# Six-layer transformer on one core: the 96 modulation slots move from TensorE to VectorE

## The reference, cut to what matters

```python
def _adaln(c, w, b):
    mod = jax.nn.silu(c) @ w + b        # (1,2048) @ (2048, 6144), for each of two layers
    shift, scale, gate = jnp.split(mod, 3, axis=-1)
```

## Time and profile before

| | |
|---|---|
| time, median of 3 runs (lowest, highest) | 4247.78 us (4247.11, 4262.5) |
| span of the profiled execution, first to last instruction | 4257.0 us |
| time of that execution outside its span | not listed |
| busy: PE, PE weight load, DVE, ACT, POOL | 3822.6, 3641.7, 2778.6, 2089.6, 599.0 us |
| mean granted TensorE clock | 0.950 of full speed |
| HBM read | 676.25 MB, 159 GB/s over the span |

### The profile page before, as it was taken

How to read it: one execution, slowest core, us unless ns; L and a number is a source line. 1 busy time by engine, 2 the same in 40 slices (tenths; PEclk the granted TensorE clock), 3 DMA queues, 4 the chain that set the end, 5 groups by cost and what they waited for, 6 DMA issues and landing times.

```text
span 4257.0 us, 80674 instructions
## 1 busy us (share of the span) xinstructions
PE 3822.6 (90%) x29682; PEld 3641.7 (86%) x29682; DVE 2778.6 (65%) x4250; ACT 2089.6 (49%) x3218; POOL 599.0 (14%) x564
## 2 busy tenths in 40 slices
PE   7999998988889886798999989889999897899997
PEld 6898888877779886798989889788989886799996
DVE  6676665566666675566667666678787774754555
ACT  5555544555545546555555544444454443443442
POOL 1011012100002201122101111223121221100000
PEclk9999999999999987899999999899999998899998
DMA  5555544444444432344555444343434342244442
GB/s 211 188 206 190 187 169 155 162 178 169 176 152 176 150 139 100 141 168 159 198 187 198 186 161 178 138 149 138 160 136 157 143 151 95 109 168 160 161 167 89
DMA packets 93571, 681.56 MB, mean 160 GB/s; under 512 B 10401, under 2 KB 10529, under 8 KB 11169
## 3 DMA queue, kind: packets, MB, share of 16 engines
q1 hardware_dynamic: 92880, 676.75, 43.6%
q0 software_dynamic: 464, 1.64, 0.1%
HBM read 676.25 MB, written 2.10 MB: 159 GB/s over the span
## 4 chain that ended last, share of the span: by engine, by line
PE 60%; DVE 15%; issue 10%; ACT 9%; POOL 4%; DVEq 1%; ACTq 0%; DMA 0%; POOLq 0%; SPq 0%
PE g L336 18%; PE g L337 17%; PE g L338 17%; DVE w_lo L1263 5%; ACT w_hi L789 4%; POOL scratch L2052 3%; PE norm_bank L349 1%; PE g L396 1%; PE g L395 1%; DVE scratch L1759 1%; ACT scratch L829 1%; ACT scratch L828 1%; PE turn_bank L375 1%; DVE scratch L1325 1%; PE g L408 1%
## 5 line engine op out<-in xcount | busy, mean ns | idle before, releaser
L1263 DVE TENSOR_TENSOR w_lo<-w_raw,w_hi 128x1024 fp32r<-128x1024 f32 x1280 | 1578.8, 1238 | 936.1 <-ACT w_hi L789 933.2
L789 ACT ACTIVATE w_hi<-w_raw 128x1024 fp32r<-128x1024 f32 x1280 | 1322.9, 1053 | 1328.4 <-PE g L338 1310.9
L336 PE MATMUL g<-p_hi,w_hi 128*128 128x256 f32 x4624 | 1346.8, 291 | 59.0 <-DVE scratch L1669 17.2
L337 PE MATMUL g<-p_lo,w_hi 128*128 128x256 f32 x4624 | 1324.3, 286 | 0.0
L338 PE MATMUL g<-p_hi,w_lo 128*128 128x256 f32 x4624 | 1323.5, 286 | 0.0
L336 PE MATMUL g<-q_hi,w_hi 128*128 128x256 f32 x3472 | 1004.5, 289 | 51.4 <-DVE q_lo L1833 14.8
L337 PE MATMUL g<-q_lo,w_hi 128*128 128x256 f32 x3472 | 991.4, 286 | 0.0
L338 PE MATMUL g<-q_hi,w_lo 128*128 128x256 f32 x3472 | 991.3, 285 | 0.0
L336 PEld LDWEIGHTS g<-p_hi,w_hi 128*128 128x128 f32 x4624 | 902.1, 195 | 74.3 <-DVE w_lo L1263 39.8
L337 PEld LDWEIGHTS g<-p_lo,w_hi 128*128 128x128 f32 x4624 | 903.4, 195 | 1.0
L338 PEld LDWEIGHTS g<-p_hi,w_lo 128*128 128x128 f32 x4624 | 902.8, 195 | 0.0
(11 more groups left out here) (339 smaller groups left out, 3750.8 us busy)
## 6 DMA issues: line engine op xcount, KB each, us to landing
w_raw<-in_slots SPq DMA_DIRECT2D x640, 1024.0 KB, 4.8
h<-in_x SPq DMA_DIRECT2D x1, 2048.0 KB, 10.9
out_h<-h SPq DMA_DIRECT2D x1, 2048.0 KB, 6.3
scratch<-in_p POOLq DMA_DIRECT2D x4, 256.0 KB, 3.8
con<-in_consts SPq DMA_DIRECT2D x1, 878.0 KB, 4.9
scratch<-in_distance POOLq DMA_DIRECT2D x1, 576.0 KB, 4.0
vec<-in_vecs SPq DMA_DIRECT2D x1, 383.0 KB, 3.2
scratch<-in_positions SPq DMA_DIRECT2D x1, 128.0 KB, 6.5
```

What stands on the lines that cost most here:

```text
L336: pe.matmul(g, wh, hi[:, k], start=n == 0, stop=False)
L337: pe.matmul(g, wh, lo[:, k], start=False, stop=False)
L789: act.activation(w_hi[k % SPLIT][:, cols], raw[k % RAW][:, cols], ACT.Copy).then_inc(hi_ready, 1)
L1263: dve.tensor_tensor(w_lo[k % SPLIT][:, cols], raw[k % RAW][:, cols], w_hi[k % SPLIT][:, cols], SUB).then_inc(lo_ready, 1)
```

## The change

The modulation slots are no longer split and PE no longer touches them. DVE multiplies each of the 8 pieces of a raw slot by the matching column of `silu(c)` (one value per partition) and sums them into `acc` over 128 partitions (`ada_half`: four pieces each, all but the slot's last linked to the next). `mod_columns` on PE sums over the partitions and now waits for `ada_summed`. In an A head, each even tick has its first half before the take and its second half at the end of the tick. In a B pair, slot 0 stands behind `b_weigh`, slot 1 ahead of the first `mod_columns`, slot 2 behind `b_y_lo`, slot 3 ahead of the take of the second gate tile. The raw buffers are handed out in the order main, main, modulation (A) and main, main, modulation, modulation (B). A load still waits for what was in its buffer before: for `lo_ready` after an ordinary slot, for `ada_used` after a modulation slot. `c_silu` replaces `ada_hl` and `ada_hz`; one short preparation step on ACT and two on DVE go. `lo_half` indexes raw buffers as `hi_ahead` does, the loop counts and the counts in GpSimd's list follow; those are left out here.

```diff
@@ -292,17 +333,57 @@
-        n_slots = t["slots"].shape[0]
-        for s in range(RAW):
-            sp.dma_start(raw[s][:], t["slots"][s]).then_inc(landed[s], 16)
-        c.k["slot"] = RAW
-        with c.loop(sp, "slots", 1, n_slots // RAW) as i:
+        kinds = []
+        def load(index, kind="main"):
+            s = c.k.get("raw", 0) % RAW
+            if len(kinds) >= RAW:
+                if kinds[-RAW] == "main":
+                    sp.wait_ge(lo_ready, c.at("slot", -kinds[1 - RAW:].count("main")) * 2)
+                else:
+                    sp.wait_ge(ada_used, c.at("ada", -kinds[1 - RAW:].count("ada")))
+            sp.dma_start(raw[s][:], t["slots"][index]).then_inc(landed[s], 16)
+            kinds.append(kind)
+            c.next("raw")
+            c.next("slot" if kind == "main" else "ada")
+        def run(first, n):
             for s in range(RAW):
-                sp.wait_ge(lo_ready, c.at("slot", -RAW + 1) * 2)
-                sp.dma_start(raw[s][:], t["slots"][i * RAW + s]).then_inc(landed[s], 16)
-                c.next("slot")
+                load(first + s)
+            if n >= 2 * RAW:
+                with c.loop(sp, "run", 1, n // RAW) as i:
+                    for s in range(RAW):
+                        load(i * RAW + (first + s))
+            for s in range(n // RAW * RAW, n):
+                load(first + s)
+        def a_head(at):
+            for main, ada in zip((0, 3, 6, 9), (1, 4, 7, 10)):
+                load(at + main)
+                load(at + main + 2)
+                load(at + ada, "ada")
+        def b_pair(at):
+            for two in (0, 4):
+                load(at + two + 1)
+                load(at + two + 3)
+                load(at + two, "ada")
+                load(at + two + 2, "ada")
+        def heads(first):
+            a_head(first)
+            with c.loop(sp, "a_heads", 1, A_HEADS) as i:
+                a_head(i * 12 + first)
+        heads(0)
+        run(96, 34 + 9)
+        b_pair(139)
+        with c.loop(sp, "b_pairs", 1, B_PAIRS) as i:
+            b_pair(i * 8 + 139)
+        run(203, 34 + 36 + 34)
+        heads(307)
+        run(403, 34 + 113 + 88 + 2)
...
@@ -381,31 +462,14 @@
             w = slot()
             tile(w, range(SLOT), hi, lo, range(SLOT), arriving=arriving)
-        def mod_slot(m, fresh=False):
-            w = slot()
-            pe.wait_ge(tile_taken, c.at("tile", 0 if fresh else -1))
-            g = G[c.bank][0:2, 0:SEQ]
-            c.bank ^= 1
-            for b in range(8):
-                if b == 4:
-                    second_half()
-                k = 8 * (m % 2) + b
-                cols = slice(b * SEQ, (b + 1) * SEQ)
-                pe.matmul(g, ada_hl[:, k], w_hi[w][:, cols], start=b == 0, stop=False)
-                last = pe.matmul(g, ada_hz[:, k], w_lo[w][:, cols], start=False, stop=b == 7)
-                if b == 3:
-                    last.then_inc(half_used, 1)
-            last.then_inc(tile_done, 1)
-            c.next("tile")
         def mod_columns():
-            pe.wait_ge(tile_taken, c.at("tile"))
+            pe.wait_ge(ada_summed, c.next("ada_sum"))
+            pe.wait_ge(tile_taken, c.at("tile", -1))
             g = G[c.bank]
             c.bank ^= 1
             for e in range(2):
-                last = pe.matmul(g[:, e:e + 1], acc[0:2, e * P:(e + 1) * P], K("ones", 1, rows=2), start=True, stop=True)
+                last = pe.matmul(g[:, e:e + 1], acc[:, e * P:(e + 1) * P], K("ones", 1), start=True, stop=True)
             last.then_inc(tile_done, 1)
             c.next("tile")
...
@@ -478,8 +542,6 @@
                         pe.matmul(bS[s][:, 0:P], q[:, 0:P], k[:, 0:P], start=True, stop=True)
                         pe.matmul(bS[s][:, P:3 * P], q[:, P:SEQ], k, start=True, stop=True).then_inc(scored, 1)
                     c.next("score_read", 2)
-                if j % 2 == 0:
-                    mod_slot(j // 2)
                 if j in (3, 7):
                     mod_columns()
...
@@ -499,11 +561,9 @@
         def b_pair(hi, lo, prev):
             c.bank = 0
-            mod_slot(0, fresh=True)
             w = slot()
             for n in range(3):
-                tile(w, range(4 * n, 4 * n + 4), c_hi, c_lo, range(4))
-            mod_slot(1)
+                tile(w, range(4 * n, 4 * n + 4), c_hi, c_lo, range(4), fresh=n == 0)
             if prev:
                 b_turn_weights()
             norm_pair(K("avg_128"), [bsq[:, 0], bsq[:, 1]])
...
@@ -514,12 +574,10 @@
             if prev:
                 b_mix()
             mod_columns()
-            mod_slot(2)
             rotate(bq[:, 2], K("swap_64"), 3)
             norm_pair(K("avg_128"), [bsk[:, 0], bsk[:, 1]])
             square_tiles(hi, lo)
             turn([bv[:, s, n * P:(n + 1) * P] for s in range(2) for n in range(2)], tile_taken, c.at("tile", -1))
-            mod_slot(3)
             square_tiles(hi, lo)
             mod_columns()
             pe.wait_ge(roped, c.next("roped"))
...
@@ -782,11 +840,13 @@
         def hi_ahead(half, ahead=2):
-            k = c.k["slot"] + ahead - 1
+            k, r = c.k["slot"] + ahead - 1, c.k["raw"] % RAW
             cols = slice(half * HALF, (half + 1) * HALF)
             if half == 0:
-                act.wait_ge(landed[k % RAW], c.fours("slot", ahead - 1) * 16)
-            act.activation(w_hi[k % SPLIT][:, cols], raw[k % RAW][:, cols], ACT.Copy).then_inc(hi_ready, 1)
+                act.wait_ge(landed[r], c.fours("raw", 0) * 16)
+            act.activation(w_hi[k % SPLIT][:, cols], raw[r][:, cols], ACT.Copy).then_inc(hi_ready, 1)
+            if half == 1:
+                c.next("raw")
         def factor_pair():
             act.wait_ge(factor_ready, c.at("norm"))
...
@@ -884,6 +944,8 @@
         def a_head(y, i, prev, first):
             for j in range(8):
+                if j % 2 == 0:
+                    c.next("raw")
                 tick(read=True)
                 if j < 4:
                     act.activation(sqh[:, j % 2], qs[:, j % 3], ACT.Square).then_inc(sq_head, 1)
...
@@ -905,8 +967,6 @@
                     sigmoid(zc[:, j - 6], clamped, c.next("clamped"))
                 if j == 7:
                     a_softmax()
-                if j % 2 == 0:
-                    tick()
                 if j in (3, 7):
                     c.next("tile")
...
@@ -936,11 +996,10 @@
             turned(b_sm[:, 1], bR[:, 0:384])
         def b_pair(y, i, prev):
-            tick()
+            c.next("raw", 2)
             tick(3, read=True)
             for n in range(3):
                 squares(bsq[:, n], bq[:, n])
-            tick()
             if prev:
                 b_turned()
             factor_pair()
...
@@ -1273,16 +1330,31 @@
             c.bank ^= 1
             return g
-        def mod_tick(m):
-            begin()
-            g = take()[0:2]
-            if m % 2 == 0:
-                dve.tensor_copy(acc[0:2], g).then_inc(tile_taken, 1)
-            else:
-                dve.wait_ge(tile_taken, c.at("tile", -1))
-                dve.tensor_tensor(acc[0:2], acc[0:2], g, ADD).then_inc(tile_taken, 1)
-            lo_half(1)
+        def ada_next():
+            at = c.k["raw"] % RAW, c.fours("raw", 0) * 16
+            c.next("raw")
+            return at
+        def ada_half(at, m, half):
+            r, value = at
+            if half == 0:
+                dve.wait_ge(landed[r], value)
+            for b in range(4 * half, 4 * half + 4):
+                w = raw[r][:, b * SEQ:(b + 1) * SEQ]
+                k = 8 * (m % 2) + b
+                if k == 0:
+                    last = dve.tensor_scalar(acc[:], w, c_silu[:, 0:1], None, MUL)
+                else:
+                    last = dve.scalar_tensor_tensor(acc[:], w, c_silu[:, k:k + 1], acc[:], MUL, ADD)
+                if b < 7:
+                    link(last)
+            if half == 1:
+                last.then_inc(ada_used, 1)
+                dve.wait_ge(ada_used, c.next("ada"))
+                if m % 2:
+                    dve.sem_inc(ada_summed, 1)
         def mod_columns(i, at):
             two = lambda base: bass.ds(i * 4 + (base + at), 2)
...
@@ -1383,7 +1455,11 @@
         def a_head(y, i, prev, first, jl):
             for j in range(8):
+                if j % 2 == 0:
+                    ada = ada_next()
                 begin()
+                if j % 2 == 0 and not (first and j == 0):
+                    ada_half(ada, j // 2, 0)
                 g = take()
                 if first and j == 0:
                     factor()
...
@@ -1430,7 +1506,9 @@
                         last = dve.tensor_reduce(tiny[:, 5 + 2 * s:6 + 2 * s], sm[:, s, P:384], AX.X, MAX, negate=True)
                     last.then_inc(maxed, 1)
                 if j % 2 == 0:
-                    mod_tick(j // 2)
+                    if first and j == 0:
+                        ada_half(ada, 0, 0)
+                    ada_half(ada, j // 2, 1)
                 if j in (3, 7):
```

(25 more changed lines are left out.)

60 lines of the change are left out of this document (48 added, 12 removed).

## The result

| | before | after |
|---|---|---|
| median (lowest, highest) of 4 runs each | 4252.98 us (4247.11, 4262.5) | 4382.12 us (4377.64, 4384.88) |
| ratio, 95% interval | | 1.0302 (1.0282 to 1.0322) |
| span of the profiled execution | 4257.0 us | 4382.6 us |
| mean granted TensorE clock | 0.950 | 0.917 |

The change makes the kernel 129 us slower. The page after: span, busy times, the chain by engine, and two groups, the linked multiply-adds and ACT's copies; they answer to the earlier trace rows.

The account below looks back on a forecast made before the run. PE was taken to bound A heads, and the order of waits between PE and DVE to bound B pairs. A +40, B +93 and preparation -1 gave +132 us on 4247.8: 4380 us, range 4270 to 4480.

Parts of the forecast that it names:

- A +40: All A heads together: 14 at +3 us each, less 2 us for the layers' first heads, +40 us.
- B +93: Eight B pairs, each +11.6 us longer than the 49.4 us before: +93 us.
- the pair's 61: Period of a B pair: 56.2 us at full clock, 61 with low clock behind PE's waits; bounds 55 and 66.
- the low clock: B pair: slower PE work behind three waits adds 1.5, 1.2 and 2.5 us on the path.
- What is removed: PE loses 1.9 us a modulation slot, 7.7 an A head, 7.3 a B pair; an A head needs PE 57.2 us.
- 8 x 0.63 = 5.0 us: DVE's cost per modulation slot: eight linked multiply-adds at layer C's linked pace of 0.63 us, 5.0 us.
- Rival (b): Links between DVE's multiply-adds cost nothing, 3.2 us a slot: about 4216 us; chance 0.07.
- Forecast waits of DVE: A head: behind exponentials 2.9, load 3.6, rotation 1.5, half of slot 4 3.7 to 4.9, load for slot 8 1.3 us.
- the raw buffers bite too: B pair: next queries' load queues behind a modulation slot's load; DVE idles from 29.2 to 35.9 us.
- (a): Whole kernel: PE is relieved and DVE keeps up, 182 us less, 4066 us; chance 0.06.
- (c): Loads hide and the clock holds: A head 62.9, B pair 56.5 us, +25 us, 4273 us; chance 0.2.
- (d): Low clock also behind every A head's 5 us wait and before its next slot 0: 4477 us; chance 0.12.

Follow-up runs that it names:

- e_early: Changed kernel with A's raw buffers ordered main, modulation, main, and one modulation half ahead of each tick's split in A heads: 4239.48 us, ratio 0.9962.
- e_twochain: Changed kernel with two interleaved sums, each multiply-add awaiting the one before the last, and mod_columns adding both: 4323.55 us, ratio 1.0162.
- e_order: Changed kernel with raw buffers in the A layers alone handed out main, modulation, main: 4294.52 us, ratio 1.0098.
- e_bwarm2: Changed kernel with useless matmuls ahead of PE's three waits in each B pair, the third batch reaching up to the scores: 4328.82 us, ratio 1.0152.
- e_spread: Changed kernel with A's buffers main, modulation, main, modulation halves behind ticks 0 to 5 and a whole slot behind tick 6: 4274.40 us, ratio 1.0049.
- e_bload: Changed kernel with only the order of layer B's loads changed, so no soon-needed slot inherits a long-held modulation buffer: 4374.15 us, ratio 1.0258.
- e_bdefer: Changed kernel with PE's two mod_columns of a B pair moved behind the first gate slot and behind the scores: 4350.20 us, ratio 1.0222.
- e_bboth: Changed kernel with both B's load order changed and PE's two mod_columns moved behind the first gate slot and the scores: 4297.01 us, ratio 1.0075.
- e_alldve: Changed kernel with e_early's order in A and e_bboth's in B, all 96 modulation slots on VectorE: 4156.66 us, ratio 0.975.
- e_bwarm: Changed kernel with useless matmuls ahead of PE's three waits in each B pair, the third batch ending 3.76 us before mod_columns: 4374.70 us, ratio 1.0283.

## Why the prediction was right, point by point

**The total** came as forecast: 4380 against 4382.12 us, +132 against +129 by the medians. The terms came less well and made up for each other: A +40 was about +15 (9.0 + 0.9 + 5.1), B +93 was about +101 (11.3 + 89.9), and +9.4 behind them was not foreseen. That the sum lies within 3 us of the measured difference is therefore luck, and so in part is the pair's 61: it was added up with the slot's cost 0.6 us too high (2.4 us a pair), the low clock 1.5 us too low and the second wait at `mod_columns` 2.4 us too long. B came out above the forecast in part because the pair of 49.4 us before, from which I reckoned, was among the long ones; the mean of seven was 48.8.

**What is removed.** PE's share was right: in e_early heads are 57.6 us, PE's own time of the forecast.

**What is added.** The term of the sum that was mis-sized most is "8 x 0.63 = 5.0 us" a slot. A linked step takes 0.52, and a whole slot 4.4 us (2.21 + 2.19, rows above). Layer C's instruction has the same shape and the same link; its scalar stands at an address that depends on the loop. Whether that makes 0.63 of it was not tested. I took the nearest row for the thing itself. 0.6 us less a slot is 2.4 us a head; half of it came back at the rotation (2.69 us of waiting, forecast 1.5), and the head is 66.7 instead of 68 us, some 20 of the 25 us by which A's +40 was too high. The rest need not be the change's: in the profile before, three heads of layer 3 were already 66.7 to 68.1 us long, together 7.7 us above the others. DVE was also less busy than forecast, 49.2 us of the head (74%) instead of 54.2 (about 80%): 2.4 us by the shorter step, and part of the rest because DVE's waits for its own last sum (0.22 to 0.30 us behind each half) are not busy time.

**Rival (b), free links.** e_twochain tells it: 0.40 us unlinked against 0.52 linked, so to await the instruction just before costs 0.12 us, half of what I charged; and with the faster pace the time was 4323.55, not 4216: the heads came to 63.6 us on average where the rival had 60.8, and next to nothing of it came through in B, where the two products added to each `mod_columns` took 1.7 us a pair. The Trainium skill's rule ("VectorE: DVE Perf Modes", section "The DRAIN you can't avoid"), that a semaphore after each instruction of a chain costs nothing extra, holds for e_twochain, where each instruction signals and 0.40 is the pace of the unlinked pair in the earlier trace rows; it does not hold where each awaits the one just before, at 0.52.

**The A head.** Forecast waits of DVE 2.9, 3.6, 1.5, 3.7 to 4.9 and 1.3 us; measured 2.81, 3.29, 2.69, 4.74 and 1.07. PE idle at the output norm: some 5, measured 4.47. The releasers were as forecast: a load at ticks 2 and 6. e_order shows these waits to be a chain: opening the first also shrinks the later ones, in part by the clock.

**The B pair.** Forecast 61, measured 61.4. PE's waits: 3.9, 8.7 and 10, measured 3.92, 8.36 and 7.57; DVE's for the next queries 6.7, measured 5.50. The low clock: 1.5 + 1.2 + 2.5 = 5.2 us, measured 6.7 by e_bwarm2. What I had wrong is that "the raw buffers bite too" is a cost that adds: the load and the queue bind at the same instant; the order of loads alone gives nothing back, and the queue alone 3.7 us, about what the scores gain by their clock.

**Rivals (a), (c), (d).** (a), that DVE keeps up, falls for this kernel, yet e_early shows it to be true of the A layers with another order. (c), that loads hide and the clock holds, fell for this kernel, but its two prices were near: it put a head without waits for loads at 62.9 (e_order 61.4) and a pair at full clock at 56.5 (e_bwarm2 54.8). (d) fell as a whole, since the A heads' mean clock is 0.95 and they are 66 to 67 us long, but half of its condition came true: the granted clock did fall to 0.50 behind the output norm's wait (394 to 398 us), and it was 1.00 from 420 us to the end of the head, ahead of the next slot 0.

**What stays open.** Six kernels that leave B's order of work on PE as it is (after, e_order, e_spread, e_twochain, e_early, e_bload) have pairs of 61.4 us in their steady run, though one has 2.6 us less DVE work and one its loads in another order. Their common mark is a granted clock of 0.50 under the scores. The pairs without it are all shorter (e_bdefer 57.8, e_bwarm2 54.8, e_bboth and e_alldve 51.2), and e_bwarm, which still has it, takes 60.4. Whether it is the clock that holds the pairs at one length is not shown, since all but e_bwarm2 changed the order of work too. In e_twochain 1.7 of the 2.6 us went into the longer `mod_columns`, and PE is busy 44.2 us of the pair (after: 41.6), so what is saved need not come back as PE's idle time; why the pairs come back to 61.4 us so exactly was not tried.

## What to carry to other kernels

Work moved to an engine with idle time is paid by its place: the same 49 us of VectorE work made a head of 66.7 or of 57.6 us. Before such a move, ask three things: what stands behind the result in the in-order queue of the engine that gave the work up, which soon-needed load inherits the buffer that is now held longer, and at what clock that engine resumes after the wait that it has been given. If two waits end together, try both remedies at once before you drop either.

## What the runs showed of the hardware that I had not expected

- The same multiply-add of 128x256 float32 on DVE takes 0.52 us from start to start when each waits for the one before, 0.40 when it waits for the last but one, and 0.63 in layer C's linked pair.
- 28 more useless matmuls on PE, which filled the last 3.76 us ahead of the scores, made the kernel 46 us faster (4374.70 to 4328.82): the scores ran at 1.00 instead of 0.50 of full clock.
- Pairs of 61.4 us in six different kernels, all with 0.50 of full clock under the scores, and shorter ones (57.8, 54.8 and 51.2 us) in kernels whose scores ran at 1.00, with all of B's sums on VectorE there too.
